# VectorE adds the last unit's output to x before its feed, and TensorE sums the last two squares singly

## The reference, cut to what matters

```python
x = x + gt1[:, None, :] * (mixed @ w_out)
h = adaln(rms_norm(x, g_mlp), sh2, sc2)      # x * rsqrt(mean(x * x) + eps) * gain, then scale and shift
u = jnp.square(jax.nn.relu(h @ w_up))
x = x + gt2[:, None, :] * (u @ w_down)
```

## Time and profile before

| | |
|---|---|
| median of three runs | 1631.77 us |
| profiled execution | 1632.41 us, its span 1630.6 us |
| TensorE matmul busy | 1543.5 us (95%) |
| VectorE busy | 1214.7 us (74%) |
| ScalarE busy | 836.5 us (51%) |
| GpSimd busy | 208.9 us (13%) |
| mean granted TensorE clock | 0.97 |
| a 1 MB unit of `w_up`, median from issue to landing | 6.0 us |
| reciprocal of each norm, start | 250.2 ("m", 0), 451.9 ("a", 1), 667.5 ("m", 1), 873.0 ("p", 0), 904.8 ("e", 0), 1400.0 ("e", 1) us |

### The profile page before, as it was taken

How to read it: one execution, slowest core, us unless ns; L and a number is a source line. 1 busy time by engine, 2 the same in 40 slices (tenths; PEclk the granted TensorE clock), 3 DMA queues, 4 the chain that set the end, 5 groups by cost and what they waited for, 6 DMA issues and landing times.

```text
span 1630.6 us, 24346 instructions
## 1 busy us (share of the span) xinstructions
PE 1543.5 (95%) x9950; PEld 1289.3 (79%) x9950; DVE 1214.7 (74%) x1843; ACT 836.5 (51%) x1164; POOL 208.9 (13%) x185
## 2 busy tenths in 40 slices
PE   6899989999999998999999899999989878899998
PEld 2889888999988977899998577777767746577775
DVE  1858898888877865899996587878757784387773
ACT  3547436444444652544545556666524465356661
POOL 3250010000005000000002300034210400300020
PEclk8999999999999999999999999999988989999999
DMA  9854497999965448588881489999954631499983
GB/s 328 276 181 130 158 326 270 321 315 320 307 203 158 130 132 289 200 284 286 296 302 52 168 338 379 364 365 359 369 211 153 213 127 65 152 342 370 357 323 116
DMA packets 184927, 409.14 MB, mean 251 GB/s; under 512 B 7576, under 2 KB 136016, under 8 KB 166256
## 3 DMA queue, kind: packets, MB, share of 16 engines
q1 hardware_dynamic: 170688, 334.53, 58.5%
q0 software_dynamic: 11200, 63.49, 10.9%
q10 hardware_dynamic: 2928, 9.57, 1.5%
HBM read 397.07 MB, written 10.49 MB: 250 GB/s over the span
## 4 chain that ended last, share of the span: by engine, by line
PE 78%; DVE 12%; ACT 5%; DMA 3%; issue 2%; POOL 0%; SPq 0%; ACTq 0%; DVEq 0%; POOLq 0%
PE psum L724 75%; DVE acc L2016 3%; DVE w_lo L1993 3%; ACT w_hi L1497 1%; ACT att_room L1926 1%; DMA raw<-in_w_ada 1%; DVE tmp L2047 1%; PE psum L1225 1%; PE psum L1258 1%; DVE tmp L2233 1%; DVE h_lo L2056 1%; DVE stats L2564 1%; PE psum L1014 1%; DMA h_rows<-tmp 1%; DVE x L2508 1%
## 5 line engine op out<-in xcount | busy, mean ns | idle before, releaser
L1993 DVE TENSOR_TENSOR w_lo<-raw,w_hi 128x1024 fp32r<-128x1024 f32 x250 | 304.5, 1260 | 82.7 <-ACT w_hi L1497 82.7
L724 PE MATMUL psum<-h_hi,w_lo 128*128 128x256 f32 (+1 forms) x1280 | 338.0, 287 | 1.0 <-DVE w_lo L1993 1.0
L724 PE MATMUL psum<-h_lo,w_hi 128*128 128x256 f32 (+1 forms) x1280 | 338.4, 288 | 0.0
L1497 ACT ACTIVATE w_hi<-raw 128x2048 fp32r<-128x2048 f32 x125 | 238.7, 1911 | 93.1 <-DMA raw<-in_w_up 45.7
L724 PE MATMUL psum<-h_hi,w_hi 128*128 128x256 f32 (+1 forms) x1280 | 262.3, 297 | 7.9 <-DVE tmp L2233 5.7
L724 PEld LDWEIGHTS psum<-h_hi,w_lo 128*128 128x128 f32 x1280 | 247.9, 194 | 2.5 <-DVE w_lo L1993 1.2
L724 PEld LDWEIGHTS psum<-h_lo,w_hi 128*128 128x128 f32 x1280 | 248.1, 194 | 1.6 <-DVE h_lo L2250 0.2
L2016 DVE SCALAR_TENSOR_TENSOR acc<-raw,cond,acc 128x1024 f32<-128x1024 f32 x182 | 239.5, 1324 | 4.0
L2028 DVE TENSOR_TENSOR gu_lo<-raw,gu_hi 128x1024 fp32r<-128x1024 f32 x184 | 213.3, 1221 | 33.5 <-ACT gu_hi L1511 33.5
L724 PEld LDWEIGHTS psum<-h_hi,w_hi 128*128 128x128 f32 x1280 | 198.2, 195 | 31.5 <-issue 18.5
L1511 ACT ACTIVATE gu_hi<-raw 128x2048 fp32r<-128x2048 f32 x96 | 178.2, 1905 | 0.0
(11 more groups left out here) (269 smaller groups left out, 2588.0 us busy)
## 6 DMA issues: line engine op xcount, KB each, us to landing
raw<-in_w_ada SPq DMA_DIRECT2D x48, 1024.0 KB, 6.5
raw<-in_w_mod SPq DMA_DIRECT2D x48, 1024.0 KB, 5.7
raw<-in_w_in SPq DMA_DIRECT2D x34, 1024.0 KB, 5.7
raw<-in_w_up SPq DMA_DIRECT2D x32, 1024.0 KB, 6.0
raw<-in_w_down SPq DMA_DIRECT2D x32, 1024.0 KB, 5.6
raw<-in_moe_wg SPq DMA_DIRECT2D x32, 1024.0 KB, 7.9
raw<-in_moe_wu SPq DMA_DIRECT2D x32, 1024.0 KB, 8.1
dn_raw<-in_moe_wd SPq DMA_DIRECT2D x32, 1024.0 KB, 7.2
```

Of the source, the lines that this page charges most:

```text
L724: return e.matmul(o, lhs, rhs, start=start, stop=stop, skip_group_check=True)
L1497: e.activation(flat_unit(w_hi[:, split_slot(u)]), raw[:, slot, :], ACT.Copy).then_inc(*w_rounded.on(u))
L1993: e.tensor_tensor(flat_unit(w_lo[:, split_slot(u), k]), raw[:, slot, part], plain(flat_unit(w_hi[:, split_slot(u), k])), ALU.subtract).the ...
```

## The change

Three things change. TensorE gets `sum_last`, which waits for the two last squares one by one and sums each with matmuls of its own; it takes the place of the last `sum_pair` at six norms (all but the first and the one behind the first experts). GpSimd no longer adds the last pair at these norms. And VectorE's last `add_x` before ("m", 0), ("a", 1), ("m", 1) and ("p", 0) now stands ahead of `feed`, while the column work that `feed` began with stays in its old place; at the first three the feed has work in it.

```diff
+            def sum_last(stage, n):
+
+                for t in (6, 7):
+                    e.wait_ge(*copied.at("sq", stage, t))
+                    for i in range(n // P):
+                        d = mm(psum[:, 6, i:i + 1], tbuf(4 + t % 4)[:, i * P:(i + 1) * P], mean[:, 0:1], False, False)
+                d.then_inc(*turned.on("sq", stage, 6))
...
                 idle(4, 2)
-                sum_pair(stage, 6, False, S)
+                sum_last(stage, S)
                 close_norm(g0 + 24)
...
-                    if j < 8:
+                    if j < 7:
                         feed(g0 + 17 + j)
+                    if j == 7:
+                        columns(g0 + 23)
+                    if j == 8:
+                        feed(g0 + 24)
...
-                    if i < 32:
+                    if i < 31:
                         feed(g0 + 25 + i)
+                    if i == 31:
+                        columns(g0 + 55)
+                    if i == 32:
+                        feed(g0 + 56)
                 columns(g0 + 56)
                 norm_scale(("a", 1) if l == 0 else ("p", 0))
...
-                    if j >= 5:
+                    if 5 <= j < 8:
                         square_pair(("m", l), 2 * (j - 5))
...
-                        if what == "down" and g == 3:
+                        if what == "down" and g == 3 and j < 3:
                             square_pair(nxt, 2 * j)
...
-            for t in range(0, DT, 2):
+            for t in range(0, DT - 2, 2):
                 square_pair(("e", 0), t)
...
-            for t in range(0, DT, 2):
+            for t in range(0, DT - 2, 2):
                 square_pair(("e", 1), t)
```

More of the change, by code:

```diff
@@ L1099, in layer @@
                 idle(4, 2)
-                sum_pair(nxt, 6, False, n)
+                sum_last(nxt, n)
                 norm(nxt)
@@ L1157, in tensor_program @@
             idle(4, 2)
-            sum_pair(stage, 6, False, S2)
+            sum_last(stage, S2)
             norm(stage)
```

## The result

The changed kernel took 1635.27 us (median of 16 runs, 1629.97 to 1638.42), the kernel before 1632.05 us (16 runs, 1629.46 to 1633.44). The ratio is 1.0017, with a 95% interval of 1.001 to 1.0025: slower by about 2.8 us. The forecast was 1638.2 us, and the time lies just under its range of 1635.5 to 1641.0. The profiled execution took 1635.73 us with a span of 1633.9 us; that of before had 1632.41 and 1630.6.

A forecast was written before the change was run, and what follows sets the result against it. TensorE, busy for 95% of the span, was taken as the bound. Terms -0.68 + 1.76 + 3.23 + 0.90 + 0.90 + 0.28 = +6.4 us gave 1638.8 profiled, 1638.2 us median, range 1635.5 to 1641.0.

The forecast's parts named there:

- ("m", 0): At this norm the reciprocal comes earlier, at 249.52 against 250.20: -0.68 us, bounds 0 and -1.0.
- ("a", 1): At this norm the 6.23 us feed behind the adds delays the reciprocal from 451.90 to 453.66: +1.76 us.
- ("m", 1): At this norm the feed behind the adds delays the reciprocal from 667.54 to 670.77: +3.23 us, at most +3.8.
- Single sums at ("p", 0) and ("e", 0): At these norms the filler hid GpSimd's add, so 4 more matmuls cost +0.90 us at each.
- "Does the delay stay?": From norm ("m", 1) to the MLP's end, a product that starts late ends late; shifted loads cost nothing.
- The clock: Behind ("a", 1) and ("m", 1) the half clock comes again; term zero, 1.5 us per norm either side.
- "half clock longer": Rival: longer pauses at ("a", 1) and ("m", 1) lengthen the half clock, 1.5 us each, 1641.2 us; chance 0.09.
- The step that failed: At ("e", 1) the sum starts at about 1398.9 with 4 more records, making the root later: +0.28 us.
- "they come as late as I say and a later stage ends on time": Sign of being wrong: reciprocals at ("a", 1) and ("m", 1) 7.0 and 8.0 us behind the product, yet later stage on time.

The follow-up runs named there:

- x4_single_e1: The kernel before, with TensorE's single sums and without GpSimd's last add at ("e", 1) alone: 1627.12 us, ratio 0.9969.
- x7_pairs_only: The changed kernel, with GpSimd adding the last pair again at ("p", 0) and ("e", 0): 1632.07 us, ratio 1.0007 to the kernel before.
- x5_split_feed: The changed kernel, with only the two `w_lo` behind the last adds and the `acc` ahead of them: 1624.96 us, ratio 0.9966 to the kernel before.
- x6_split_feed_pairs: The changed kernel with the edits of x5_split_feed and x7_pairs_only together: 1623.46 us, ratio 0.9954 to the kernel before.
- x9_filled_pause: The changed kernel, with unused matmuls in TensorE's pause at ("a", 1) and ("m", 1): 1632.87 us, ratio 1.0012 to the kernel before.
- the three comparisons above: x4_single_e1 against the kernel before, 5.1 us; the changed kernel against itself with GpSimd held, 3.4, and with loads held, 4.7 us.
- x1_order_only: The kernel before, with VectorE's last adds moved ahead of the feed and the sums still in pairs: 1638.32 us, ratio 1.0040.

## Why the forecast was wrong

Step by step:

- ("m", 0): forecast -0.68, measured 5.97 - 6.68 = -0.71 us. Right, but see below for the 6.68.
- ("a", 1): forecast +1.76, measured 7.07 - 5.31 = +1.76 us. Right, the saved 0.44 us of the `acc` beside GpSimd's add included. The rule of the Trainium skill, page "SBUF — State Buffer" (section "SBUF: two separate sides"), by which the loser at the shared port is blocked for a whole instruction, would have given up to 0.3 us less, and the trace does not agree with it in size. The add began at 442.73, 0.10 us ahead of the `acc`, so it was not quite inside it, as the prediction has it: 0.64 us of it ran beside the `acc`, and that cost 0.44.
- That these two agree to 0.03 us is in part luck. The changed kernel has 5.97 and 7.07 us in all five traces of its code at these norms, but the code of before has 6.68 and 5.31 us in one trace and 6.08 and 4.57 in another (x4_single_e1). Against the second, the terms would be -0.11 and +2.50.
- ("m", 1): forecast +3.23, measured 8.14 - 4.73 = +3.41 us. Right: four `acc` took 5.02 us to the next instruction where I had taken 4.85.
- Single sums at ("p", 0) and ("e", 0): forecast +0.90 each. At ("p", 0) measured 5.52 - 4.63 = +0.89 us. At ("e", 0) it is +0.66 behind the filler's end, since the sum of before already took 1.05 us there. For both, x7_pairs_only and the step from x5_split_feed to x6_split_feed_pairs give 1.6 and 2.0 us. Right in size.
- "Does the delay stay?" Until ("e", 0) it does; the changed kernel is even 8.6 us late there.
- The clock, taken as zero with 1.5 us on either side: nothing more at ("a", 1), but about +1.3 us at ("m", 1), by the 1.36 us that x9_filled_pause gives back between two norms. This was the rival "half clock longer", at one norm of two; it is inside the 1.5 us that I had allowed, and with the limits said above.
- **The step that failed: "At ("e", 1) the sum started at 1399.05, 0.12 us behind the filler's end ... root 0.28 us later, +0.28 us".** On TensorE it came to +0.06 us: the reciprocal 1.12 us behind the filler's end, against 1.06 before. But I looked at TensorE alone. The edit also takes a wait out of GpSimd's queue, and behind it there stand the weights of the first expert. They were split 6 us earlier in relation to the norm, the loads left the path of the `h_rows` store, and the gather and the product that waits for it came 3.05 us earlier; with the clock, the three comparisons above put it at -4.4 us. The same weights stand behind the last pair at ("e", 0), and no run shows a gain there. The trace of before says why: the loads were issued by 913.09 us and the store of `h_rows` began at 918.16, 5 us behind them, so the store took 2.9 us and the gather waited for its addresses already. At ("e", 1) the loads were issued 0.3 and 0.7 us ahead of the store.

The terms as measured are -0.71 + 1.76 + 3.41 + 0.89 + 0.66 + 0.06 + 1.3 - 4.4 = +3.0 us, against +2.8 (1.6 to 4.1 by the interval) from the ratio and +3.3 between the two profiled executions. A match this close is in part luck, since the terms are not that firm. What is left over in the table of stretches (-1.07 before the first norm, +2.0 of ("e", 0), -1.49 up to ("e", 1)) is in stretches whose length also differs between kernels that are the same there: 26.93 to 29.00 us up to the first reciprocal, and 171.33 us up to ("e", 1) in x1_order_only against 172.78 in the kernel before, whose trace has a low stretch of the granted clock there that the other lacks. Whether the low stretch behind the +2.0 us at ("e", 0) comes from the change is open: with pairs the stretch between the norms is 31.83 or 31.84 us in four kernels, but 33.40 in x7_pairs_only; with single sums it is 32.63 and 32.74 in two and 34.75 to 36.15 in four.

My text had named as its test that "they come as late as I say and a later stage ends on time", and that is what happened. I had asked who waits for each engine that is made later, and not what starts earlier where an engine is relieved. The page of before pointed to it: its chain had 3% of DMA, and `h_rows<-tmp` was 1% of it by line.

The page "DMA: Bandwidth & Descriptors" of the Trainium skill (section "Queues, rings and completion order") says that each DMA engine serves its queues in turn, one packet each. The traffic of the kernel before agrees with that for a part of the store's time only; q1 carries SyncE's loads and q10 the store. From 1409 to 1413 us:

```profile
q1 hardware_dynamic: 152, 1.13, 89.0%
```

and from 1413 to 1417 us:

```profile
q1 hardware_dynamic: 126, 0.97, 68.8%
q10 hardware_dynamic: 129, 0.51, 30.9%
```

In the second stretch the two queues do move packet for packet, 126 against 129 (the page's packet holds several descriptors; whether it is the same as a packet of the trace no run shows), and the store gets half the bytes, as its packets are half as large (4 KB against 8). But in the first stretch not one packet of the store moves, though its first half was issued at 1409.03: the first starts at about 1413.3 us, 4.3 us behind the issue, against 0.8 us in the changed kernel. So the longer part of the store's delay is a wait for its first turn, and why that comes so late no run here shows.

## What to carry to other kernels

An instruction taken from an engine's queue can be worth more than its own wait when other work stands behind it: follow that queue to its next instructions, the slots they free and the transfers these start, also where the engine is 13% busy. Then compare the times of issue: loads 0.3 to 0.7 us ahead of the store cost 3 us here, and loads 5 us ahead of it nothing. When adds are moved ahead of filling work, move only as much of it behind them as fits between the adds and the next thing that the same engine owes; here 2.35 us fitted and 6.2 and 7.3 us did not. A later start of TensorE can cost more than its length if its pause grows, since what follows may run at 1.2 GHz: here about 1.3 us at one norm of two, by one pair of traces.

## What the runs showed of the hardware that I had not expected

A store of two 512 KB pieces on ScalarE's queue took 8.7 us while two 1 MB loads of SyncE's queue were out, and 2.6 us without them. TensorE's pause of 5.39 us was followed by about 6 us at a granted clock of 0.50 in the changed kernel and by 4.4 to 4.7 us in three other kernels with the same pause; the pause of 3.14 us at ("a", 1) was followed by low clock no longer than before, until 3.8 us behind the reciprocal (455.5 us), against 4.9 us (456.8) in the kernel before. An `acc` of 128x1024 elements took 1.72 us beside a GpSimd add that overlapped it by 0.64 us, and 1.28 or 1.29 us alone.
